# Second block: the S5 mixer ahead of block attention in the side stream, block attention's inputs as plain fp32 products, its gates in a ring slot

## The chip, the cores and the metric

One NeuronCore of a Trainium2 chip runs the whole program. The metric is the device time of one execution in microseconds. The kernel before was timed in three runs.

## The reference, cut to what matters

Two transformer layers (the first block) are followed by one second block; all is fp32, with 256 rows of 1024. The change lies in the second block's mixer:

```python
proj = x @ w_in                               # 1024 -> 1792 RWKV + 1536 MoBA + 512 S5 + 3 x 1024 gates
y_a = rwkv7_mixer(proj[..., :OFF_MOBA], ...)  # a recurrence over 256 positions, 8 heads of 64
y_b = moba_attention(q, k, v)                 # 8 heads; one block of 256, so causal attention with ALiBi
y_c = s5_mixer(proj[..., OFF_SSM:OFF_GATE], ...)   # 32 groups, complex diagonal recurrence, then a GLU
gates = sigmoid(proj[..., OFF_GATE:] + gate_b)     # three gates of 1024 columns
merged = g_rwkv * (y_a @ w_up_rwkv) + g_moba * (y_b @ w_up_moba) + g_ssm * (y_c @ w_up_ssm)
y = merged @ w_out
```

After it come a layer norm, a router and 32 experts.

## The kernel before, in words

For the second block each engine runs three programs woven into one list (`weave`, L149): the RWKV stream, the side stream and a stream of gates ahead. The weaver takes one step (up to a `yield STEP`) of each in turn, in this order; I call that a round and count rounds from the second block's first input product. The list is fixed when the program is built, and every engine works it off strictly in order, so an instruction that waits holds up all behind it. PSUM banks 0 to 3 belong to RWKV, 4 to 6 to the side stream, 7 to the gates.

**Input products.** `proj` is computed in pieces of 256 columns (1 MB of weights). Thirteen are split products, the units (`units_tensor`): ACT writes a rounded copy of the weights (L291), DVE the remainder (L301), and PE multiplies in three passes (L242 to L244). They are the 7 RWKV pieces and the 6 of block attention (queries and keys by columns, values by rows), one a round in rounds 1 to 13. Gates, S5's two input pieces and the products up from a branch are plain fp32 products (`product_cols`, L266).

**Weights.** Every piece is loaded by SP into a ring of `RING` = 4 slots (`WeightRing`). Piece n waits for the use of piece n - 4.

**RWKV.** Its vectors are made beside the units: DVE L1990 to L2013 with exponentials on ACT (L1933, L1937). `b` and `k` (L2005, L2006) wait for a unit whose weights lay in the same memory; `bend` and `kend` (L2012, L2013) follow the last exponential. Then the scan goes over two tiles t of 128 positions: transposes (L2068) in rounds 14 to 17, G with the pair masks (L2074 to L2077, DVE L2232) in 18 to 21, a triangular inverse by products per head (L2045) up to round 33, four steps (L2140 to L2148) in 35 to 38, the chunks (L2159), the output. Tile 1 does the same in rounds 44 to 73. The last product up (RWKV's) and the output product (L736) follow.

**Side stream.** After the units comes block attention in rounds 14 to 27, two groups of four heads: scores (L2379), DVE mask and maximum (L2416, L2423, L2430), exponential on ACT (L887), transposes (L900), the product with the values (L1106). Its product up is in rounds 28 and 29. S5 has its inputs in rounds 30 and 31 and its preparation in 32 to 35: small DVE rows L2640 to L2674 and four transposed pairs (L2524). Eight parts of three rounds each follow, to round 60. For a part, ACT makes an angle (L2575), POOL turns it into the period (L2488, L2490), ACT takes sine and cosine (L2582 to L2587); PE multiplies in (L2510); DVE rotates (call it A, L2688 to L2695), scans (B, L2703) and rotates back (C, L2707 to L2712); PE multiplies out (L2544). The GLU, S5's gates and its product up end the stream in round 67.

**Gates ahead.** After 13 empty steps, block attention's gates run in rounds 14 to 17 and RWKV's in 18, 21, 24 and 27; ACT reads each with a sigmoid (L1801). The result of block attention's stands in `merged`, RWKV's in its own tile.

**POOL** shifts the RWKV inputs (L1627 to L1631) beside the units, then makes distances, pair masks (a memset and 56 selects, L349), `time` and `number`; when block attention is over, it issues S5's loads (L84) and then its part of the angles.

## Time and profile before

| what | us |
|---|---|
| three runs: median (lowest to highest) | 1974.78 (1971.98 to 1976.24) |
| profiled execution, its own time | 1968.7 |
| its span, first to last instruction | 1967.5 |
| busy over the span: PE, DVE, ACT, POOL | 1535.4, 1113.0, 732.7, 147.4 |
| first unit of the second block to first gate | 985 to 1100 |
| block attention and its product up (rounds 14 to 29) | 1099 to about 1220 |
| S5's preparation, parts, then gates and product up | 1241 to 1459 |
| RWKV alone, then the output product and experts | 1462 to the end |

PE is the busiest engine, at a mean granted clock of 0.871. In the timeline each row is a run of like instructions on one engine: its start, its length, line and operation, and in brackets how long the engine had stood idle before it, with the instruction that released it. What ends an idle stretch is read there; busy time alone does not tell it.

### The profile page before, as it was taken

The page shows a single profiled execution, that of the slowest core. Times are in us where ns is not written, and L with a number is a line of the kernel's source. Part 1 is how long each engine was busy: PE and PEld are TensorE (multiplying, and loading weights), DVE is VectorE, ACT ScalarE, POOL GpSimd, SP SyncE. Part 2 cuts the span into 40 slices and gives each one's busy share as a digit, 9 for nine tenths or more (in the row PEclk, how much of TensorE's full clock was granted, in tenths as well). Part 3 has the DMA queues.
Part 4 walks back from the last instruction along what each step waited for, and adds up shares of the span by engine and source line. Part 5 has one row for each costly group of instructions (what it writes and reads, how often), then busy time and mean ns, then how long its engine had stood idle before and what let it go on. Part 6 is the DMA issues. An engine that isn't in the chain of part 4 may idle for free. (4 is left out here: it accounts for less than half of the span.)

```text
span 1967.5 us, 21292 instructions
## 1 busy us (share of the span) xinstructions
PE 1535.4 (78%) x8755; PEld 1276.7 (65%) x8755; DVE 1113.0 (57%) x1457; ACT 732.7 (37%) x926; POOL 147.4 (7%) x226
## 2 busy tenths in 40 slices
PE   2963465999696436899878989787896559999995
PEld 2952455999595335799777878645784446666663
DVE  6756635656675662544456341588124467676675
ACT  2302324444332340554344322332200146666661
POOL 2000001000100000000078000121001000000000
PEclk9975777999797668999989989778987779999997
DMA  8960014878582002555443313100222329999971
GB/s 302 348 241 0 1 44 171 280 250 292 167 285 66 0 0 86 172 173 196 146 121 116 120 65 97 44 1 0 86 86 68 128 86 338 343 344 344 343 296 64
DMA packets 134567, 310.30 MB, mean 158 GB/s; under 512 B 6223, under 2 KB 99750, under 8 KB 114886
## 3 DMA queue, kind: packets, MB, share of 16 engines
q1 hardware_dynamic: 130310, 299.18, 43.3%
q0 software_dynamic: 3584, 8.71, 1.7%
q8 instruction: 69, 1.13, 0.2%
q10 hardware_dynamic: 576, 1.05, 0.2%
q14 instruction: 28, 0.23, 0.0%
HBM read 307.87 MB, written 1.05 MB: 157 GB/s over the span
## 5 line engine op out<-in xcount | busy, mean ns | idle before, releaser
L301 DVE TENSOR_TENSOR mlp_weights_lo<-weights,mlp_weights_hi 128x2048 fp32r<-128x2048 f32 x64 | 146.3, 2291 | 55.9 <-ACT mlp_weights_hi L291 55.9
L242 PE MATMUL bank<-mlp_in_hi,mlp_weights_hi 128*128 128x256 f32 x512 | 147.2, 288 | 14.9 <-DVE mlp_weights_lo L301 14.9
L3177 DVE TENSOR_TENSOR expert_pair_lo<-weights,expert_pair_hi 128x2048 fp32r<-128x2048 f32 x53 | 119.9, 2290 | 64.0 <-ACT expert_pair_hi L3168 64.0
L243 PE MATMUL bank<-mlp_in_lo,mlp_weights_hi 128*128 128x256 f32 x512 | 146.7, 286 | 0.0
L244 PE MATMUL bank<-mlp_in_hi,mlp_weights_lo 128*128 128x256 f32 x512 | 146.6, 286 | 0.0
L291 ACT ACTIVATE mlp_weights_hi<-weights 128x2048 fp32r<-128x2048 f32 x64 | 121.8, 1910 | 49.7 <-issue 44.4
L242 PE MATMUL bank<-expert_pair_hi,x_block_hi 128*128 128x512 f32 x280 | 114.0, 407 | 5.3 <-issue 5.3
L242 PEld LDWEIGHTS bank<-mlp_in_hi,mlp_weights_hi 128*128 128x128 f32 x512 | 100.2, 196 | 16.7 <-DVE mlp_weights_lo L301 15.7
L244 PE MATMUL bank<-expert_pair_hi,x_block_lo 128*128 128x512 f32 x280 | 110.2, 393 | 0.0
L243 PE MATMUL bank<-expert_pair_lo,x_block_hi 128*128 128x512 f32 x280 | 110.0, 393 | 0.0
L266 PE MATMUL bank<-hT,weights 128*128 128x256 f32 x448 | 101.7, 386 | 0.7 <-ACT merged L1801 0.6
L243 PEld LDWEIGHTS bank<-mlp_in_lo,mlp_weights_hi 128*128 128x128 f32 x512 | 100.3, 196 | 1.1
L244 PEld LDWEIGHTS bank<-mlp_in_hi,mlp_weights_lo 128*128 128x128 f32 x512 | 100.0, 195 | 0.0
L242 PE MATMUL bank<-mlp_weights_hi,hidden_hi 128*128 128x512 f32 x256 | 100.0, 391 | 0.0
L243 PE MATMUL bank<-mlp_weights_lo,hidden_hi 128*128 128x512 f32 x256 | 100.0, 390 | 0.0
L244 PE MATMUL bank<-mlp_weights_hi,hidden_lo 128*128 128x512 f32 x256 | 99.6, 389 | 0.0
L538 DVE SCALAR_TENSOR_TENSOR ada<-weights,cond,ada 128x2048 f32<-128x2048 f32 x42 | 98.6, 2347 | 1.4
L3168 ACT ACTIVATE expert_pair_hi<-weights 128x2048 fp32r<-128x2048 f32 x53 | 99.2, 1907 | 0.0
L266 PEld LDWEIGHTS bank<-hT,weights 128*128 128x128 f32 x448 | 85.1, 192 | 14.0 <-issue 2.2
L855 DVE TENSOR_TENSOR hidden_lo<-mlp_raw,hidden_hi 128x512 fp32r<-128x512 f32 x32 | 22.1, 692 | 98.1 <-ACT hidden_hi L831 98.1
L3281 DVE TENSOR_TENSOR y_sorted<-bank,y_sorted 128x512 f32 (+1 forms) x70 | 48.4, 692 | 46.1 <-PE bank L3213 45.7
L825 ACT ACTIVATE mlp_raw<-bank 128x512 f32<-128x512 f32 x32 | 19.1, 598 | 126.3 <-PE bank L244 126.3
(728 smaller groups left out, 3760.9 us busy)
## 6 DMA issues: line engine op xcount, KB each, us to landing
weights<-in_w_ada SPq DMA_DIRECT2D x48, 1024.0 KB, 5.3
weights<-in_w_in SPq DMA_DIRECT2D x45, 1024.0 KB, 5.5
weights<-in_expert_w_gate SPq DMA_DIRECT2D x35, 1024.0 KB, 5.6
weights<-in_w_up SPq DMA_DIRECT2D x32, 1024.0 KB, 5.5
weights<-in_w_down SPq DMA_DIRECT2D x32, 1024.0 KB, 6.0
weights<-in_expert_w_up SPq DMA_DIRECT2D x18, 1024.0 KB, 6.9
weights<-in_expert_w_down SPq DMA_DIRECT2D x18, 1024.0 KB, 7.3
expert_raw<-in_expert_w_up SPq DMA_DIRECT2D x17, 1024.0 KB, 6.6
```

What stands on the lines that cost most here:

```text
L242: pe.e.matmul(out, lhsT[0], rhs[0], start=start, stop=False)
L243: pe.e.matmul(out, lhsT[0], rhs[1], start=False, stop=False)
L244: return pe.e.matmul(out, lhsT[1], rhs[0], start=False, stop=stop)
L266: ins = pe.e.matmul(bank[:, j * SEQ:(j + 1) * SEQ], w[:, k, j * P:(j + 1) * P], xT[:, k, :], start=k == 0, stop=k == tiles - 1)
L291: act.e.activation(self.of(n)[0], ring.view(name), ACT.Copy).then_inc(*act.mark(*self.key, "high", n))
L301: dve.e.tensor_tensor(lo, ring.view(name), hi.bitcast(F32), SUB).then_inc(*dve.mark(*self.key, "low", n))
L538: dve.e.scalar_tensor_tensor(part, ring.view(name), s.cond[:, k:k + 1], part, MULT, ADD).then_inc(*dve.mark(*name))
L825: act.e.activation(s.raw, as_cols(c.up_banks.of("up", l, n)), ACT.Relu).then_inc(*act.mark("read", "up", l, n))
L855: dve.e.tensor_tensor(lo, s.raw, hi.bitcast(F32), SUB).then_inc(*dve.mark("hidden low", l, n))
L3168: act.e.activation(pair[0][:, :, i * D_EXPERT:(i + 1) * D_EXPERT], expert_raw(s, kind, n), ACT.Copy).then_inc(*act.mark("expert", "high", ...
L3177: dve.e.tensor_tensor(pair[1][:, :, part], expert_raw(s, kind, n), pair[0][:, :, part].bitcast(F32), SUB).then_inc(*dve.mark("expert", "lo ...
L3281: dve.e.tensor_tensor(part, c.banks[4 + 2 * (n % 2) + half].unsqueeze(1), part, ADD).then_inc(*dve.mark("expert", "added", n, half))
```

## The change

S5 becomes the first user of the side stream. The units are now 9, the 7 of RWKV and the 2 of S5. S5's preparation takes rounds 10 to 12, its first product in is in 13, and its eight parts end in round 36, beside scan tile 0. GLU and product up are in rounds 37 to 40. The six inputs of block attention are plain fp32 products from the ring, rounds 41 to 46, and block attention runs in rounds 47 to 60 beside scan tile 1, its product up in 61 and 62. From round 63 on RWKV is alone. All twelve gates go ahead in the order S5, RWKV, block attention, one in every second round from 10 to 32. S5's stand in `merged`; block attention's stand in ring slot 3, which the ring gives away at the last unit and goes on with 3 slots. POOL issues S5's loads after the first shift group, makes `time` and `number` before the shifts, the pair masks between its angle parts 0 and 1, the distances after S5. `b` and `k` wait for unit 7 instead of 11. The experts' loads also wait for the last product merged from block attention. In the changed program lines stand lower: L266 becomes L275, L2524 L2552, L2510 L2538, L2544 L2571, L1801 L1820, L2068 L2087, L349 L365, L2488 L2516.

```diff
...
-        self.order.append((name, piece))
+        slot = self.free.pop(0)
+        self.free.append(slot)
+        self.place[name] = slot, len(self.pieces_of[slot]), piece
+        self.pieces_of[slot].append(name)
+        self.order.append(name)
+    def give(self, slot):
+        self.free.remove(slot)
+        return self.pieces_of[slot][-1]
     def view(self, name):
...
-        return self.order[n][1][0](self.slots[n % RING])
+        slot, _, piece = self.place[name]
+        return piece[0](self.slots[slot])
...
-            if n >= RING:
-                yield from sp.wait_ge("used", *self.order[n - RING][0])
-            sp.e.dma_start(view(self.slots[n % RING]), source).then_inc(self.full[n % RING], 16)
-            n += 1
+            name = self.order[done]
+            slot, n, (view, source) = self.place[name]
+            if n:
+                yield from sp.wait_ge("used", *self.pieces_of[slot][n - 1])
+            sp.e.dma_start(view(self.slots[slot]), source).then_inc(self.full[slot], 16)
...
@@ -1586,13 +1602,17 @@
     return pieces
-def second_constants_gpsimd(c, s):
+def distances_gpsimd(c, s):
     pool = c.join.pool
     for t in range(TT):
         pool.e.iota(s.distance[:, t, :], pattern=[[-1, SEQ]], base=t * P, channel_multiplier=1,
                     allow_small_or_imprecise_dtypes=True).then_inc(*pool.mark())
         select(pool, s.distance[:, t, :], ALU.is_ge, 1e34, t * P, [[-1, SEQ]], 1)
...
+def pair_masks_gpsimd(c, s):
+    pool = c.join.pool
     pool.e.memset(s.pair, 1.0).then_inc(*pool.mark())
     for kind, block in ((0, C), (1, C), (2, C), (3, 16), (4, 16)):
...
+    pool.also("pair masks")
...
     pool.e.memset(s.chunk_start.rearrange("p (n c) -> p n c", c=C)[:, :, 0:1], 0.0).then_inc(*pool.mark("chunk starts"))
+    pool.e.iota(s.time, pattern=[[1, SEQ]], base=0, channel_multiplier=0,
+                allow_small_or_imprecise_dtypes=True).then_inc(*pool.mark())
+    pool.e.iota(s.number, pattern=[[0, 1]], base=0, channel_multiplier=1).then_inc(*pool.mark("numbers"))
...
@@ -1629,6 +1650,8 @@
             pool.e.tensor_scalar(s.shift_tmp, s.shift_tmp, s.v["rwkv_mu_2"][:, k:k + 1], None, MULT).then_inc(*pool.mark())
             pool.wait_own()
             pool.e.tensor_tensor(shifted[k], s.shift_tmp, s.z[:, k, 1:SEQ + 1], ADD).then_inc(*pool.mark("rw shifted", k))
+        if n == 0:
+            s5_loads_gpsimd(c, s)
...
-    s.input_weights = Pairs(c, c.join, ("in 2",), s.pieces["rwkv"] + s.pieces["moba"], s.input_pairs)
+    s.input_weights = Pairs(c, c.join, ("in 2",), s.pieces["rwkv"] + s.pieces["ssm"], s.input_pairs)
...
@@ -1706,9 +1729,7 @@
 def input_units(s):
-    return [*((COLS, s.z[:, 2 * n:2 * n + 2, 1:SEQ + 1]) for n in RWKV_ORDER),
-            *((COLS, s.qkT[:, 2 * n:2 * n + 2, :]) for n in range(4)),
-            *((ROWS, s.mb_v[:, :, 256 * n:256 * n + 256]) for n in range(2))]
+    return [*(s.z[:, 2 * n:2 * n + 2, 1:SEQ + 1] for n in RWKV_ORDER), *(s.u[:, 2 * n:2 * n + 2, :] for n in range(2))]
...
 def units_vector(c, s):
+    s.gates_after = c.ring.give(RING - 1)
...
     dve.e.tensor_copy(s.chunk_decay.rearrange("p k n -> p (k n)"), chunks(s.rw_work)[:, :, C - 1]).then_inc(*dve.mark("rw log", "inverse"))
     yield STEP
     yield STEP
-    yield from dve.wait_ge("in 2", "product", 11)
+    yield from dve.wait_ge("in 2", "product", 7)
     yield from dve.wait_ge("rw exp", "inverse")
...
         yield STEP
     dve.wait_own()
-    yield from dve.wait_ge("second constants")
+    yield from dve.wait_ge("pair masks")
...
-    yield from add_branch_vector(c, s, dve, banks, 0, 2, s.rwkv_gates, s.b[:, 0:2, :])
...
+    yield from add_branch_vector(c, s, dve, banks, 0, 1, s.rwkv_gates, s.b[:, 0:2, :])
...
+    s.mb_pT, s.mb_tmp = mem.new("mb_pT", 4, 2, SEQ), mem.new("mb_tmp", 2, SEQ)
+    s.mb_gates = k_tiles(8)(c.ring.slots[RING - 1])
...
+    return [*((COLS, s.qkT[:, 2 * n:2 * n + 2, :]) for n in range(4)), *((ROWS, s.mb_v[:, :, 256 * n:256 * n + 256]) for n in range(2))]
...
+def moba_inputs_tensor(c, s):
+    pe, banks = c.side.pe, c.side_banks
+    for n, (kind, _) in enumerate(moba_inputs(s)):
+        name = "mb in", n
+        c.ring.next(name, s.pieces["moba"][n])
+        yield from c.ring.wait_ge(pe, name)
+        bank = yield from banks.take(pe, *name)
+        product = product_cols if kind == COLS else product_rows
+        product(pe, bank, c.hT, c.ring.view(name), KT).then_inc(*pe.mark(*name))
+        pe.also("used", *name)
+        yield STEP
...
@@ -2455,32 +2502,13 @@
...
 def s5_angles_gpsimd(c, s):
     pool = c.start.pool
     for part in range(8):
+        if part == 1:
+            pair_masks_gpsimd(c, s)
...
-    yield from pe.wait_ge("read", "s5 u", 1)
-    yield STEP
+    yield from pe.wait_ge("read", "in 2", 8)
     yield from s5_in_tensor(s, pe, banks, 0)
...
@@ -2750,62 +2777,59 @@
 def side_branches_tensor(c, s):
     pe, banks = c.side.pe, c.side_banks
     yield from units_tensor(c, s)
+    yield from s5_tensor(c, s)
+    yield from add_branch_tensor(c, s, pe, banks, 2, s.s5_yT)
+    yield from meet(c, "tensor", "s5", "side")
+    yield from moba_inputs_tensor(c, s)
+    for n in range(4):
+        yield from pe.wait_ge("read", "mb in", n)
     for h0 in (0, 4):
         yield from moba_tensor(c, s, h0)
     yield from add_branch_tensor(c, s, pe, banks, 1, s.mb_yT)
-    yield from meet(c, "tensor", "moba", "side")
-    yield from s5_u_tensor(c, s)
-    yield from s5_tensor(c, s)
-    yield from gates_tensor(c, s, pe, banks, 2)
-    yield from add_branch_tensor(c, s, pe, banks, 2, s.s5_yT)
...
-    yield from meet(c, "scalar", "moba", "side")
-    yield from s5_u_scalar(c, s)
-    yield from s5_scalar(c, s)
-    yield from act.wait_ge("branch", 2)
-    yield from gates_scalar(c, s, act, banks, 2, s.s5_gates)
...
 def side_branches_vector(c, s):
     dve, banks = c.side.dve, c.side_banks
     yield from units_vector(c, s)
+    yield from s5_vector(c, s)
+    yield from add_branch_vector(c, s, dve, banks, 2, None, s.merged, None)
+    yield from meet(c, "vector", "s5", "side")
+    for n in range(6):
+        yield STEP
     for h0 in (0, 4):
         yield from moba_vector(c, s, h0)
-    yield from add_branch_vector(c, s, dve, banks, 1, None, s.merged, None)
-    yield from meet(c, "vector", "moba", "side")
-    for n in range(2):
-        yield STEP
-    yield from s5_vector(c, s)
-    for n in range(4):
-        yield STEP
-    yield from add_branch_vector(c, s, dve, banks, 2, 1, s.s5_gates, s.s5_tmp)
...
-AHEAD_STEPS = 13
+    yield from add_branch_vector(c, s, dve, banks, 1, 2, s.mb_gates, s.mb_tmp)
+AHEAD_STEPS, SPACES = 9, 1
...
 def gates_ahead_tensor(c, s):
     for _ in range(AHEAD_STEPS):
         yield STEP
-    for branch, spaces in ((1, 0), (0, 2)):
-        yield from gates_tensor(c, s, c.ahead.pe, c.ahead_banks, branch, spaces)
+    for branch in (2, 0, 1):
+        yield from gates_tensor(c, s, c.ahead.pe, c.ahead_banks, branch, SPACES)
 def gates_ahead_scalar(c, s):
+    act = c.ahead.act
     for _ in range(AHEAD_STEPS):
         yield STEP
-    for branch, gates, spaces in ((1, s.merged, 0), (0, s.rwkv_gates, 2)):
-        yield from gates_scalar(c, s, c.ahead.act, c.ahead_banks, branch, gates, spaces)
+    for branch, gates in ((2, s.merged), (0, s.rwkv_gates), (1, s.mb_gates)):
+        if branch == 1:
+            yield from act.wait_ge("used", *s.gates_after)
+        yield from gates_scalar(c, s, act, c.ahead_banks, branch, gates, SPACES)
...
 def expert_loads_sync(c, s):
     sp, ring = c.start.sp, c.ring
     sources = {kind: c.a[f"expert_w_{kind}_2"].rearrange("a e (p k) n -> (a e) p (k n)", p=P) for kind in KINDS}
-    for name, _ in ring.order[-RING:]:
-        yield from sp.wait_ge("used", *name)
+    for names in ring.pieces_of:
+        yield from sp.wait_ge("used", *names[-1])
+    yield from sp.wait_ge("merged", 1, 6)
...
     yield from shifts_gpsimd(c, s)
-    second_constants_gpsimd(c, s)
-    yield from meet(c, "gpsimd", "moba", "side")
-    s5_loads_gpsimd(c, s)
     yield from s5_angles_gpsimd(c, s)
+    yield from meet(c, "gpsimd", "s5", "side")
+    distances_gpsimd(c, s)
```

Three places show how the lists move. On PE, the rows behind the last unit before (mb_qkT are queries and keys; L2068 is RWKV's first transpose; L266 a gate):

```order
L2068 MATMUL bank0<-identity,rw_AR_324 128x128 [waits rw_scalar,rw_vector,rw_tensor]
L2068 MATMUL bank0<-identity,rw_AR_324 128x128 x3
L2379 MATMUL bank5<-mb_qkT_359 128x128 [waits join_scalar]
L2379 MATMUL bank5<-mb_qkT_359 128x128
L2379 MATMUL bank6<-mb_qkT_359 128x128 [waits join_scalar]
L2379 MATMUL bank6<-mb_qkT_359 128x128
L266 MATMUL bank7<-hT_49,weights1 128x256 [waits weights1_full]
L266 MATMUL bank7<-hT_49,weights1 128x256 x15
L2068 MATMUL bank1<-identity,rw_bend_327 128x128 x4
L266 MATMUL bank7<-hT_49,weights2 128x256 [waits ahead_scalar,weights2_full]
```

And the rows behind the last unit in the changed program (s5_bb and s5_cc are S5's matrices, L2538 its product in):

```order
L275 MATMUL bank7<-hT_49,weights0 128x256 [waits weights0_full]
L275 MATMUL bank7<-hT_49,weights0 128x256 x15
L2552 MATMUL bank4<-identity,s5_bb0_388 128x128 [waits join_scalar,side_vector]
L2552 MATMUL bank4<-identity,s5_bb0_388 128x128 x3
L2552 MATMUL bank5<-identity,s5_bb1_389 128x128 [waits join_scalar]
L2552 MATMUL bank5<-identity,s5_bb1_389 128x128 x3
L2552 MATMUL bank6<-identity,s5_cc0_391 128x128 [waits join_scalar]
L2552 MATMUL bank6<-identity,s5_cc0_391 128x128 x3
L2552 MATMUL bank4<-identity,s5_cc1_392 128x128 [waits side_scalar]
L2552 MATMUL bank4<-identity,s5_cc1_392 128x128 x3
L275 MATMUL bank7<-hT_49,weights1 128x256 [waits ahead_scalar,weights1_full]
L275 MATMUL bank7<-hT_49,weights1 128x256 x15
L2538 MATMUL bank5<-s5_u_367,s5_bT0_380 128x256 [waits side_scalar]
L2538 MATMUL bank6<-s5_u_367,s5_bT1_381 128x256
L2538 MATMUL bank5<-s5_u_367,s5_bT0_380 128x256 [waits side_tensor]
L2538 MATMUL bank6<-s5_u_367,s5_bT1_381 128x256
L2087 MATMUL bank0<-identity,rw_AR_324 128x128 [waits rw_vector,rw_scalar,rw_tensor,side_tensor]
```

Between a gate and RWKV's first transpose there now stand S5's transposes, a second gate and its first products in, each with a wait of its own.

On ACT, the same place in the changed program (L2627 reads S5's transposes, L1956 is RWKV's last exponential, L2602 the angle, L2609 to L2614 sine and cosine):

```order
L2627 ACTIVATE s5_cT1_383<-bank4 128x512 [waits side_tensor]
L1820 ACT_TABLE_LOAD
L1820 ACTIVATE merged_251<-bank7,columns_247 128x256 [waits ahead_tensor]
L1820 ACTIVATE merged_251<-bank7,columns_247 128x256
L1956 ACT_TABLE_LOAD
L1956 ACTIVATE rw_work_355<-rw_work_355 128x1024 [waits rw_vector]
L2602 ACTIVATE distance_241<-time_244,s5_th_370 128x256 [waits side_vector]
L2602 ACTIVATE distance_241<-time_244,s5_th_370 128x256
L2609 ACT_TABLE_LOAD
L2609 ACTIVATE s5_sin0_401<-distance_241 128x512 [waits start_gpsimd]
L2610 ACTIVATE s5_cos0_402<-distance_241 128x512
L2612 ACTIVATE s5_cos0_402<-s5_cos0_402 128x512 [waits side_scalar]
L2614 ACTIVATE s5_cos0_402<-s5_cos0_402,ones 128x512 [waits side_scalar]
L2201 ACTIVATE scan_W_333<-bank0 128x8x64 [waits rw_scalar,rw_tensor,rw_vector]
```

Before, L1937 (now L1956) stood ahead of the first gate's read; now it stands behind the second, and S5's first angle behind it.

On POOL, the rows behind the shifts before:

```order
L1592 IOTA distance_241 128x256
L349 AFFINE_SELECT distance_241<-distance_241 128x256 [waits join_gpsimd]
L1596 MEMSET pair_masks_242 128x640
L349 AFFINE_SELECT pair_masks_242<-pair_masks_242 128x32 [waits join_gpsimd] x24
L349 AFFINE_SELECT pair_masks_242<-pair_masks_242 128x16 [waits join_gpsimd] x32
L1609 IOTA time_244 128x256
L1611 IOTA number_245 128x1
L84 DMA s5_b_re_383<-in_ssm_b_re_2 128x16x16 [waits side_scalar,side_vector,side_tensor]
L84 DMA s5_b_im_384<-in_ssm_b_im_2 128x16x16
...
L2488 TENSOR_SCALAR s5_sin0_400<-distance_241 128x512 [waits side_scalar]
```

and in the changed program:

```order
L2516 TENSOR_SCALAR s5_sin0_401<-distance_241 128x512 [waits side_scalar]
L2518 TENSOR_TENSOR distance_241<-distance_241,s5_sin0_401 128x512 [waits start_gpsimd]
L1616 MEMSET pair_masks_242 128x640
L365 AFFINE_SELECT pair_masks_242<-pair_masks_242 128x32 [waits join_gpsimd] x24
L365 AFFINE_SELECT pair_masks_242<-pair_masks_242 128x16 [waits join_gpsimd] x32
L2516 TENSOR_SCALAR chunk_start_243<-distance_241 128x512 [waits side_scalar]
L2518 TENSOR_TENSOR distance_241<-distance_241,chunk_start_243 128x512 [waits start_gpsimd]
```

The pair masks now stand between the two angle parts instead of ahead of all of S5's work.

## Rows read from the trace of the kernel before

**Rows 1.** Windows: stretch, length, busy us (instructions) PE, PEld, DVE, ACT, POOL, clock, DMA.

```profile
1072.00:1099.00 27.00, 23.80 (x192) 23.19 (x193) 17.21 (x13) 11.29 (x11) 13.77 (x32) 1.00 0.51 157
1099.00:1244.00 145.00, 134.51 (x752) 118.33 (x752) 43.94 (x99) 41.24 (x85) 3.90 (x4) 0.94 0.30 91
1261.00:1386.00 125.00, 100.10 (x600) 66.51 (x600) 100.42 (x163) 37.30 (x65) 26.04 (x16) 0.75 0.00 1
```

**Rows 2.** Timeline of PE: first chunk product of scan tile 1 (start us, us, what).

```profile
1462.18 1.79 PE L2159 MATMUL bank<-scan_state,scan_N 128*128 128x64 f32 x8 [1.49 <-DVE scan_N L2283]
```

**Rows 3.** Timeline of ACT: results of units 8 and 12 read.

```profile
1071.72 0.60 ACT L1765 ACTIVATE mb_qkT<-bank 128x512 f32<-128x512 f32 x1 [1.34 <-PE bank L244]
...
1097.58 0.60 ACT L1765 ACTIVATE mb_v<-bank 128x512 f32<-128x512 f32 x1 [1.04 <-PE bank L244]
```

**Rows 4.** Timeline of PE: two plain products, of block attention's and of RWKV's gates.

```profile
1100.24 8.86 PE L266 MATMUL bank<-hT,weights 128*128 128x256 f32 x32
...
1135.79 7.17 PE L266 MATMUL bank<-hT,weights 128*128 128x256 f32 x32
```

**Rows 5.** Timelines of DVE and PE: first and last row of S5's preparation.

```profile
1240.91 0.17 DVE L2640 TENSOR_TENSOR s_mag<-columns,s_dt 128x16 f32<-128x16 f32 x1
...
1254.18 0.61 DVE L2674 TENSOR_SCALAR s_cc<-s_c_im,group_odd 128x256 f32<-128x256 f32 x2
...
1254.85 1.97 PE L2524 MATMUL bank<-identity,s_bb 128*128 128x128 f32 x8 [7.92 <-DVE s_cc L2674]
```

**Rows 6.** Timeline of ACT: the last exponential, a gate's read, a table load.

```profile
1095.47 1.06 ACT L1937 ACTIVATE rw_work<-rw_work 128x1024 f32<-128x1024 f32 x1 [3.05 <-DVE rw_work L2008]
...
1109.14 0.84 ACT L1801 ACTIVATE merged<-bank,columns 128x256 f32<-128x256 f32 x2 [7.46 <-PE bank L266]
1109.99 1.28 ACT L887 ACT_TABLE_LOAD   x1
1111.29 0.40 ACT L887 ACTIVATE mb_scores<-mb_scores,mb_negmax 128x128 f32<-128x128 f32 x1
```

**Rows 7.** Timelines of ACT and POOL: the first angle, turn and last cosine.

```profile
1260.05 0.90 ACT L2575 ACTIVATE distance<-time,s_th 128x256 f32<-128x256 f32 x2
...
1263.05 1.26 POOL L2490 TENSOR_TENSOR distance<-distance,s_sin 128x512 f32<-128x512 f32 x1
...
1266.19 0.72 ACT L2587 ACTIVATE s_cos<-s_cos,ones 128x512 f32<-128x512 f32 x1
```

**Rows 8.** Timeline of DVE: A's first row, C's first and last row; kend.

```profile
1281.97 0.69 DVE L2688 TENSOR_TENSOR s_br<-bank,chunk_start 128x512 f32<-128x512 f32 x1
...
1289.99 0.68 DVE L2707 TENSOR_TENSOR s_br<-chunk_start,s_gr 128x512 f32<-128x512 f32 x1
...
1292.03 0.69 DVE L2712 TENSOR_TENSOR s_gi<-chunk_start,s_gi 128x512 f32<-128x512 f32 x1
...
1097.71 1.22 DVE L2013 TENSOR_TENSOR rw_kend<-rw_k_in,rw_work 128x1024 f32<-128x1024 f32 x1
```

**Rows 9.** Timeline of PE: a part's products out and in, at either clock.

```profile
1280.43 1.06 PE L2544 MATMUL bank<-s_br,s_cT 128*32 128x256 f32 x2 [3.85 <-DVE s_gi L2712]
...
1353.42 0.62 PE L2544 MATMUL bank<-s_br,s_cT 128*32 128x256 f32 x2
...
1361.71 2.31 PE L2510 MATMUL bank<-s_u,s_bT 32*128 32x256 f32 x8
```

**Rows 10.** Timeline of PE: a scan product per head, at either clock.

```profile
1349.91 3.58 PE L2045 MATMUL bank<-scan_N,scan_PP 128*128 128x128 f32 x16 [6.36 <-DVE scan_N L2247]
...
1356.15 2.05 PE L2045 MATMUL bank<-scan_PP,scan_N 128*128 128x128 f32 x16
```

**Rows 11.** Timeline of PE: transposes of block attention, second group.

```profile
1191.36 1.10 PE L900 MATMUL bank<-identity,mb_scores 128*128 128x128 f32 x8 [3.02 <-DVE mb_scores L2430]
```

**Rows 12.** Instructions of line L349: duration ns min/median/max, first and last start us.

```profile
L349 POOL TENSOR_SCALAR_AFFINE_SELECT pair_masks<-pair_masks x56: 198/212/2532, 1059.3 to 1087.2; 128x16 f32<-128x16 f32 x32, 128x32 f32<-128x32 f32 x24
```

**Rows 13.** Page, DMA issues: KB each, us to landing.

```profile
weights<-in_w_in SPq DMA_DIRECT2D x45, 1024.0 KB, 5.5
```

More of the change, by code:

```diff
@@ L267, in product_cols, with product_rows @@
                               start=k == 0, stop=k == tiles - 1)
+    return ins
+def product_rows(pe, bank, xT, w, tiles, width=256):
+    for t in range(TT):
+        for k in range(tiles):
+            ins = pe.e.matmul(bank[:, t * width:(t + 1) * width], xT[:, k, t * P:(t + 1) * P], w[:, k, :], start=k == 0, stop=k == tiles - 1)
     return ins
@@ L1660, in group_odd_vector @@
     dve = c.side.dve
[L1661 removed]
+    yield from dve.wait_ge("numbers")
     dve.e.tensor_scalar(s.number, s.number, 4, 1, ALU.arith_shift_right, ALU.bitwise_and).then_inc(*dve.mark())
@@ L1758, in units_scalar @@
     act, units = c.join.act, input_units(s)
-    for n, (kind, dst) in enumerate(units):
+    for n, dst in enumerate(units):
         if n + 1 < len(units):
@@ L2228, in scan_vector @@
     dve.wait_own()
-    yield from dve.wait_ge("second constants")
+    yield from dve.wait_ge("pair masks")
     for h in range(HEADS):
@@ L2457, in s5_memory @@
     s.glu = [mem.new(f"s5_glu{n}", 4, SEQ) for n in range(2)]
-    s.s5_gates, s.s5_tmp = mem.new("s5_gates", 8, SEQ), mem.new("s5_tmp", 2, SEQ)
-def s5_u_tensor(c, s):
-    pe, banks = c.side.pe, c.side_banks
-    for n in range(2):
-        name = "s5 u", n
-        c.ring.next(name, s.pieces["ssm"][n])
-        yield from c.ring.wait_ge(pe, name)
-        bank = yield from banks.take(pe, *name)
-        product_cols(pe, bank, c.hT, c.ring.view(name), KT).then_inc(*pe.mark(*name))
-        pe.also("used", *name)
-        yield STEP
-def s5_u_scalar(c, s):
-    act = c.side.act
-    for n in range(2):
-        yield from act.wait_ge("s5 u", n)
-        act.e.activation(s.u[:, 2 * n:2 * n + 2, :], as_cols(c.side_banks.of("s5 u", n)), ACT.Copy).then_inc(*act.mark("read", "s5 u", n))
-        yield STEP
 def s5_angles_gpsimd(c, s):
@@ L2602, in s5_scalar @@
     yield from act.wait_ge("s5 cycles")
-    yield from act.wait_ge("second constants")
+    yield from act.wait_ge("numbers")
     yield from act.wait_ge("rw run")
```

58 lines of the change are left out of this document (28 added, 30 removed).

## The prediction, made before the changed kernel was run

> **What bounds the kernel now.** I read the windows by stage first, then PE's timeline from the first gate to the last chunk, then what ended each wait there. While gates stand beside the scan and block attention, PE is full: 134.5 of 145 us, clock 0.94 [rows 1]. Beside S5's parts it isn't: 100.1 of 125 us, clock 0.75, with DVE as busy as PE. There PE waits for C, DVE's last rows of a part, before it can multiply out (idle 3.85 [rows 9]), and its own rows take longer: a product per head 3.58 us against 2.05 [rows 10]. So the change has a target: some 25 us of holes and as much of low clock beside S5, which gates could fill. The scan's last tile starts its chunks at 1462.2 [rows 2]; what follows stays as it is. I sum from the reading of unit 8, 1071.7 [rows 3], to that first chunk: 390.5 us before. A measurement of this kernel tells a difference of about 0.2%, 4 us.
>
> **Rounds 10 to 13: 44.7 us.** Before, four units took from 1071.7 to 1097.6 and the transposes began at 1099.0. Now: a gate, 7.1 us [rows 4], to 1078.8. S5's preparation waits on DVE for the last unit and takes 13.9 us [rows 5]; DVE also has RWKV's rows there, 8.0 us in 27 when I take four remainders of 2.3 from 17.2 [rows 1], and I lay 3 of them in between. PE's transposes start at 1088.8: 10 us idle. They take 3.3, the next gate ends at 1100.0 (the first after a pause took 8.86). ACT stands before that gate's result, and RWKV's last exponential and S5's first angle stand behind it: read 0.84, table 1.28, exponential 1.06 [rows 6], angle 0.9, POOL's turn 3.4, sines 2.6 [rows 7]: 1110.1. On DVE A(0), 3.8, then bend and kend, 1.2 each [rows 8]: 1116.4. PE has 4 us of S5 in this time and is idle for 12. Round 14 begins 17.4 us later than before. Below, this could be 8 (if the preparation's small rows slip between RWKV's and the exponential isn't late); above, 22.
>
> **Rounds 14 to 36: 187 us.** PE's work: ten gates 71; eight products out of 2.7 and seven in of 2.3 [rows 9], 38; the scan's twelve products per head and eight groups about as long, 20 x 1.95, 39 (one alone 2.05 [rows 10]). That is 148. The holes: out(p) stands on PE behind the RWKV product of its round, and on DVE C(p) stands behind the row that takes this product. So a wait as long as RWKV's row and C, whose four rows take 2.7 [rows 8], comes after that product whether or not a gate ran a round earlier; the trace has one of 3.85 [rows 9]. Further, in(p+1) waits for A(p), A(p) for the sines, the sines on ACT for the gate's read: 0.84 + 1.28 + 2.6 + 3.8 = 8.5 us after a gate's end, against 6 of scan work. Together up to 5.5 a part. The nearest rows, S5's parts now, show 25 idle us for some eight parts, 3.1 each. I take 4, 32 in all, and 7 for rounds 34 to 36, where no gate is left: 39. Ends: 25 and 55.
>
> **Rounds 37 to 46: 89 us.** GLU, product up, six plain inputs: ten plain products, 71, and nine groups of scan, 18. PE is full here. Against split products the six cost PE more (7.1 against 23.8/4 = 5.95 [rows 1, 4]: +7); S5's two are cheaper by 2. DVE loses four remainders of 2.3 and ACT four copies, but neither bounds.
>
> **Rounds 47 to 60: 62 us.** Block attention and scan tile 1 are now without gates. PE has some 36 us of work, 2.6 a round. Before, a round here took 6.9 (145 us for 21), 4.1 of it plain products (twelve of 7.1). Even so PE waited 3.02 for DVE's masked scores [rows 11]. With nothing to fill, each round lasts as long as its chain: product, DVE, ACT, back. I take 4.4, between 2.6 (36 us) and 6.9 (97), nearer to 3.0 plus a wait in every second round.
>
> **Rounds 61 to the chunk: 32 us.** Two halves up, 14.2, with scan rows 3.7; then G's last products and steps, 13.9, RWKV alone.
>
> Sum 44.7 + 187 + 89 + 62 + 32 = 414.7, against 390.5: +24. The clock: PE now rests in rounds 47 to 60 as it rested beside S5. If a third of 36 us of work runs at 3.58 for 2.05, that is 9 more; the first holes give 2. RWKV rows on DVE that POOL's selects held up before give 3 back. **+32 us.** Against the profiled execution, 1968.7, it is 2001; the median of the runs shown is 6 above it, so I say 2006.
>
> **What costs nothing.** S5's four loads on POOL delay its shifts by 4 us, or up to 9 if each waits its turn; the shifts are followed by 28 us of masks now [rows 12], which move away. Three slots instead of four: a load lands 5.5 us after issue [rows 13] and has at least one product of 7.1 for cover; without it, 5.5 at most twice. SP's experts wait for the last merge of block attention, about 14 us before the chunk.
>
> **A page's rule.** A table load took 1.28 us, and the next activation began 0.02 after its end [rows 6]. The Trainium skill, "ScalarE: Activation LUTs", section "What ACT_TABLE_LOAD costs", adds a drain of about 1.38 us to every switch of set. The program gains ten loads; by the page ten drains, an estimate of 14 us, would come on top; by the row none does, so I leave it out.
>
> **Rivals.** (B) **Faster, 0.22.** Gates and S5 fit: DVE is through C before PE asks, since a gate of 7.1 us lies in between. For it: 93% busy in 1099 to 1244 with gates, and S5's rows are shorter at full clock. Against: C behind RWKV's row of the same round. It decides when the idle per part falls under 1 us and block attention's round under 3.6: rounds 14 to 36 then take 160, rounds 47 to 60 50, rounds 10 to 13 35: 49 us less than my sum, 1957. With no hole at all the work is 22 + 148 + 89 + 36 + 32 = 327, and the time 1911. (C) **About the same, 0.06**: half of the holes I laid fill, 1975. (D) **POOL's masks stand in the way, 0.17.** They start behind turn 0, at about 1107.5, and take 12 (56 at the median 0.212) to 28 us (as before, beside DVE, the longest 2.5 each) [rows 12]. Angle 1's turn stands behind them: to 1139 at worst, while A(1) is wanted near 1130; PE then loses up to 11: 2017. The Trainium skill, "GPSIMD Engine Reference", section "Key points", has GpSimd share its SBUF interfaces with VectorE and contend with two-input instructions; the longest select is twelve times the median, which agrees. (E) **A ring of three makes pieces late, 0.05**: some 5 us for several pieces, 2015 to 2025. The forecast itself has 0.5.
>
> **Chances.** Faster by over 0.2%: B, 0.22 and a share of C. Same: 0.06. Slower: the forecast, D, E. The range reaches up to D with the holes' upper end, 2034, and down into B, to 1945, which leaves out its best cases.
>
> **What would show it.** Right: PE idle about 10 us before S5's transposes and 12 before the first RWKV transpose; idle of 3 to 5 us before products out, released by C; rounds 47 to 60 around 60 us at a low clock; first chunk of tile 1 near 1071.7 + 423. Wrong: this stretch at or below 390; S5's parts over 90% busy on PE; the masks' end as what releases PE; a wait for weights in the chain.

## The result and the profile after

The changed kernel takes 2017.84 us (median of four, 2014.21 to 2024.99); the kernel before 1975.51 in the same comparison. The ratio is 1.0216, interval 1.0178 to 1.0255: slower, by 42 us. The forecast was 2006, slower, range 1945 to 2034.

The profiled execution took 2014.21 us, its span 2012.6 against 1967.5. What answers to the sum of the prediction, by its own stages, are the windows of the changed kernel (stretch, length, busy us and instructions of PE, PEld, DVE, ACT, POOL, clock, DMA); the last row runs from the first unit to the first chunk of scan tile 1:

```profile
1068.90:1113.40 44.50, 20.21 (x88) 16.86 (x88) 22.79 (x61) 19.35 (x28) 10.90 (x25) 0.74 0.15 48
1113.40:1325.30 211.90, 173.51 (x914) 130.15 (x914) 96.23 (x154) 60.68 (x96) 31.44 (x49) 0.83 0.16 50
1325.30:1413.60 88.30, 83.81 (x530) 73.27 (x529) 10.45 (x18) 12.04 (x21) 1.45 (x4) 0.96 0.34 108
1413.60:1479.70 66.10, 43.74 (x321) 40.08 (x321) 36.65 (x78) 18.07 (x50) 0.00 (x0) 0.79 0.05 17
1479.70:1506.60 26.90, 26.12 (x338) 23.97 (x336) 12.84 (x23) 2.34 (x5) 0.00 (x0) 1.00 0.23 79
993.00:1506.60 513.60, 412.82 (x2649) 343.95 (x2649) 225.46 (x368) 142.31 (x234) 98.07 (x130) 0.86 0.22 70
```

The same stretch of the kernel before:

```profile
996.50:1462.20 465.70, 404.50 (x2714) 338.75 (x2714) 232.82 (x372) 137.61 (x230) 104.87 (x130) 0.90 0.24 76
```

It is 47.9 us longer. PE is busy 8.3 us more and idle 39.6 us more (100.8 against 61.2). Of the idle time 21.9 us more lie ahead of RWKV's first transpose (34.8 against 12.8) and 17.7 behind it. If each busy moment is weighted with the clock granted in it, PE's work is 367.5 us against 365.8, an estimate from the two traces: most of the 8.3 is a lower clock, hardly any of it more work. The rest of the program is as before: 506.0 us from the chunk to the end of the span, 505.3 before. PE's timeline in the changed kernel, in order: S5's first transposes, RWKV's first transpose, the gate behind it, products out of parts 0, 1, 2 (the row of 1174.42 stands between, a product in) and 7, transposes of block attention, first chunk:

```profile
1085.64 1.97 PE L2552 MATMUL bank<-identity,s_bb 128*128 128x128 f32 x8 [9.85 <-DVE s_cc L2701]
...
1113.40 1.09 PE L2087 MATMUL bank<-identity,rw_AR 128*128 128x128 f32 x4 [14.38 <-DVE rw_kend L2032]
...
1118.67 10.01 PE L275 MATMUL bank<-hT,weights 128*128 128x256 f32 x32
...
1132.56 1.06 PE L2571 MATMUL bank<-s_br,s_cT 128*32 128x256 f32 x2 [3.44 <-DVE s_gi L2739]
...
1155.72 1.06 PE L2571 MATMUL bank<-s_br,s_cT 128*32 128x256 f32 x2 [5.58 <-DVE s_gi L2739]
...
1174.42 4.17 PE L2538 MATMUL bank<-s_u,s_bT 32*128 32x256 f32 x8 [3.43 <-DVE s_gr L2719]
...
1193.18 1.06 PE L2571 MATMUL bank<-s_br,s_cT 128*32 128x256 f32 x2 [3.67 <-DVE s_gi L2739]
...
1319.98 1.06 PE L2571 MATMUL bank<-s_br,s_cT 128*32 128x256 f32 x2 [10.50 <-DVE s_gi L2739]
...
1441.26 1.97 PE L916 MATMUL bank<-identity,mb_scores 128*128 128x128 f32 x8 [11.49 <-DVE mb_scores L2477]
...
1506.62 1.87 PE L2178 MATMUL bank<-scan_state,scan_N 128*128 128x64 f32 x8
```

Every wait shown is for a row of DVE. What DVE waited for in rounds 10 to 13 stands in its own timeline (before these two rows it made b and k and the input of RWKV's last exponential, up to 1089.2) and in ACT's:

```profile
1107.03 0.69 DVE L2715 TENSOR_TENSOR s_br<-bank,s_cos 128x512 f32<-128x512 f32 x1 [17.83 <-ACT s_cos L2614]
...
1111.92 1.23 DVE L2032 TENSOR_TENSOR rw_kend<-rw_k_in,rw_work 128x1024 f32<-128x1024 f32 x1
```

```profile
1096.82 0.84 ACT L1820 ACTIVATE merged<-bank,columns 128x256 f32<-128x256 f32 x2 [5.57 <-PE bank L275]
1097.68 1.28 ACT L1956 ACT_TABLE_LOAD   x1
1098.97 1.06 ACT L1956 ACTIVATE rw_work<-rw_work 128x1024 f32<-128x1024 f32 x1
1099.93 0.89 ACT L2602 ACTIVATE distance<-time,s_th 128x256 f32<-128x256 f32 x2
```

DVE stands still for 17.8 us before A(0), with bend and kend behind it. ACT is held up by the gate's read to 1097.7, and behind that come exponential, angle, turn and sines, 9.4 us. The table load at 1097.68 is followed by its activation 0.01 us after its end, as in [rows 6].

### The profile page after: what moved, and what is told of

Same layout as the page of the kernel before. It is cut to its first block, busy times and chain, and to the rows that moved or that the text cites. A ratio compares the mean times of both kernels' runs of the same rounds, so it can differ in the third digit from the quotient of the medians.

```text
span 2012.6 us, 21151 instructions
## 1 busy us (share of the span) xinstructions
PE 1542.5 (77%) x8691; PEld 1280.2 (64%) x8691; DVE 1105.3 (55%) x1453; ACT 738.8 (37%) x932; POOL 140.5 (7%) x226
## 4 chain that ended last, share of the span: by engine, by line
PE 70%; DVE 21%; ACT 6%; issue 2%; DMA 0%; POOL 0%; DVEq 0%; ACTq 0%
PE bank L251 12%; PE bank L252 12%; PE bank L253 12%; PE bank L275 8%; PE bank L3238 6%; PE bank L752 4%; PE bank L2064 2%; PE bank L2571 2%; DVE ada L554 2%; PE bank L499 1%; PE bank L2538 1%; PE bank L608 1%; DVE conv L1332 1%; PE bank L916 1%; ACT diff_scores L903 1%
## 5 line engine op out<-in xcount | busy, mean ns | idle before, releaser
L275 PE MATMUL bank<-hT,weights 128*128 128x256 f32 x512 | 124.4, 405 | 0.2
L275 PEld LDWEIGHTS bank<-hT,weights 128*128 128x128 f32 x512 | 103.4, 205 | 20.4 <-PE bank L2538 3.1
L251 PEld LDWEIGHTS bank<-mlp_in_hi,mlp_weights_hi 128*128 128x128 f32 x512 | 100.2, 196 | 16.7 <-DVE mlp_weights_lo L317 15.7
L3306 DVE TENSOR_TENSOR y_sorted<-bank,y_sorted 128x512 f32 (+1 forms) x70 | 48.4, 692 | 46.2 <-PE bank L3238 44.5
```

The lines of the kernel that those rows point to most:

```text
L251: pe.e.matmul(out, lhsT[0], rhs[0], start=start, stop=False)
L275: ins = pe.e.matmul(bank[:, j * SEQ:(j + 1) * SEQ], w[:, k, j * P:(j + 1) * P], xT[:, k, :], start=k == 0, stop=k == tiles - 1)
L3306: dve.e.tensor_tensor(part, c.banks[4 + 2 * (n % 2) + half].unsqueeze(1), part, ADD).then_inc(*dve.mark("expert", "added", n, half))
```

## The experiments

The start of the second block drifts: its first unit began between 993 and 1012 us, whatever the kernel. The stretch from it to tile 1's first chunk does not; in the two kernels that differ only in POOL's masks it is 513.6 both times. So I read the experiments by that stretch, from one profile each, cut at RWKV's first transpose, and give the ratio beside it. The part up to the transpose agrees within 0.3 us in the six kernels that leave PE, ACT and DVE there as in the changed one (120.3 to 120.6), and in the four with plain inputs in the old order it is 100.1 to 100.2. Behind the chunk it takes 504.1 to 509.0 us to the end of the span, so a gain of a few us in the stretch need not be one of the program. None of the ratios of the seven kernels built on the changed one but that of gates_spread has an interval apart from the changed kernel's; for all others what the edit is worth rests on the stretch alone.

| kernel | to transpose | to chunk | sum | ratio to before (interval) |
|---|---|---|---|---|
| before | 102.6 | 363.2 | 465.7 | 1 |
| changed | 120.4 | 393.2 | 513.6 | 1.0216 (1.0178 to 1.0255) |
| masks_early | 120.3 | 393.3 | 513.6 | 1.0246 (1.0221 to 1.0272) |
| gates_from_14 | 111.4 | 399.2 | 510.6 | 1.0230 (1.0205 to 1.0255) |
| s5_one_round_later | 100.9 | 410.9 | 511.9 | 1.0228 (1.0195 to 1.0260) |
| side_first_dve | 120.6 | 391.0 | 511.6 | 1.0257 (1.0235 to 1.0279) |
| filled_waits | 120.3 | 396.7 | 517.0 | 1.0265 (1.0243 to 1.0287) |
| filled_where_idle | 120.4 | 386.4 | 506.8 | 1.0193 (1.0156 to 1.0231) |
| gates_spread | 120.5 | 403.9 | 524.4 | 1.0304 (1.0272 to 1.0336) |
| plain_inputs_only | 100.1 | 358.8 | 458.9 | 0.9988 (0.9964 to 1.0012) |
| s5_gates_beside_s5 | 102.6 | 359.3 | 461.9 | 0.9992 (0.9973 to 1.0012) |
| plain_and_s5_gates | 100.2 | 357.9 | 458.1 | 0.9971 (0.9944 to 0.9998) |
| both_and_filled | 100.2 | 360.6 | 460.8 | 0.9984 (0.9963 to 1.0005) |
| side_first_s5_only | 100.1 | 364.4 | 464.5 | 0.9997 (0.9980 to 1.0014) |

**masks_early**: on the changed kernel.

```diff
-        if part == 1:
-            pair_masks_gpsimd(c, s)
...
     yield from shifts_gpsimd(c, s)
+    pair_masks_gpsimd(c, s)
     yield from s5_angles_gpsimd(c, s)
```

> The changed kernel with the pair masks made on POOL right after the shifts, ahead of S5's first angle. In the changed kernel's trace they take 19.2 us between turn 0 and turn 1, and turn 1 ends at 1127.3. Chain theory: they are mostly hidden, since sine 1 stands on ACT behind a gate's read anyway; 0 to 3 us faster than the changed kernel, ratio 1.020 to 1.0216. Rival (the masks hold up turn 1 and with it the whole chain of parts): 8 to 11 us faster, 1.016 to 1.0175.

The stretch is the same to 0.1 us, and so are the waits before the products out (3.43, 5.58, 3.66, 3.43, 10.49). Rival D falls: the masks are hidden. In the changed kernel POOL has

```profile
1104.85 19.24 POOL L365 TENSOR_SCALAR_AFFINE_SELECT pair_masks<-pair_masks 128x32 f32<-128x32 f32 x56
```

against some 28 us [rows 12].

**gates_from_14**: the gates four rounds later.

```diff
-AHEAD_STEPS, SPACES = 9, 1
+AHEAD_STEPS, SPACES = 13, 1
```

> The changed kernel with all twelve gates four rounds later (rounds 14, 16 ... 36 instead of 10 ... 32). Chain theory (what costs time are waits between engines, not PE's work): ACT no longer stands before a gate's result while RWKV's last exponential and S5's first angle wait behind it, so the first RWKV transpose comes 10 to 14 us earlier after the last unit (31 to 34 us behind it instead of 44.5); the two gates that move to rounds 34 and 36 cost 14 us of work there and fill 7 to 10 us of the idle 10.5 before the last product out. Sum: 7 to 10 us faster than the changed kernel, ratio to the kernel before about 1.017. Rival (PE's work is the bound, the order of gates does not matter): no change, 1.0216.

The start gains 9.0 us and the later rounds lose 6.0: 3 us in all, not 7 to 10. What left the start is PE's work (busy 74.9 instead of 85.6 us); its idle time there did not fall, 36.5 for 34.8. Right in direction; two gates in rounds 34 and 36 fill less than I gave them (the last wait is 6.0 instead of 10.5).

**s5_one_round_later**: the same idea driven further; the new step stands in S5's program on PE, ACT and DVE alike, ahead of part 0.

```diff
-AHEAD_STEPS, SPACES = 9, 1
+AHEAD_STEPS, SPACES = 14, 1
...
     for n in range(4):
         yield from dve.wait_ge("read", "s5 T", n)
+    yield STEP
     for part in range(8):
```

> The changed kernel with S5's parts one round later and the gates from round 15 on, so that on ACT no gate's result stands before RWKV's last exponential, and on DVE bend and kend stand ahead of A(0). Chain theory: the first RWKV transpose comes 18 us earlier (first unit to transpose 102 instead of 120.4: only S5's preparation, 14 us of small DVE rows, then b, k, bend, kend and one exponential are left); from there to tile 1's first chunk it takes 400 to 404 instead of 393.2 (two gates more, most of rounds 34 to 37 filled). First unit to chunk 502 to 506 against 513.6. Rival (what the start gains comes back as waits between the parts, as with the gates four rounds later): 510 or more.

The start comes out as said, 100.9: kend comes 19.5 us earlier when ACT's queue and A(0) are not ahead of it. But 17.7 of them come back, 1.7 are left. The rival holds. Why, PE's timeline and window behind the last unit show:

```profile
1096.48 1.97 PE L2552 MATMUL bank<-identity,s_bb 128*128 128x128 f32 x8 [16.75 <-DVE s_cc L2703]
...
1104.92 0.87 PE L2087 MATMUL bank<-identity,rw_AR 128*128 128x128 f32 x3 [4.76 <-DVE rw_kend L2032]
```

```profile
1079.70:1104.90 25.20, 3.70 (x17) 3.28 (x17) 19.48 (x55) 9.94 (x16) 2.27 (x1) 0.59 0.00 0
```

Of these 25.2 us PE is idle for 21.5; in the changed kernel it was 24.3 of 44.5. So the edit moved two gates and the first product in out of this stage, to where they had to be done later, and hardly touched the holes: kend's wait is 4.8 instead of 14.4, but s_cc's is 16.8 instead of 9.9. It shows what sets the length of the stage. It does not show that the stage's holes are harmless, and no run here took them away.

**side_first_dve**: DVE's streams swapped after 14 rounds.

```diff
-    yield from weave(rwkv_branch_vector(c, s), side_branches_vector(c, s))
+    yield from weave_then_swap(14, rwkv_branch_vector(c, s), side_branches_vector(c, s))
```

> The changed kernel with the two streams on DVE in the other order from round 14 on: in each round S5's (or block attention's) rows stand ahead of RWKV's. Chain theory: C(p) no longer stands behind the row that takes RWKV's product of the same round, so the idle time of PE before a product out falls from 3.4 to 5.6 us to 0 to 2; RWKV's rows come 2.7 to 3.9 us later and take some of it back. 5 to 12 us faster than the changed kernel, ratio 1.0155 to 1.019. Rival (C follows the scans B closely and its own length is what PE waits for): idle before products out unchanged, no change or slower by up to 10.

Two waits before products out are left (1.86, 5.42), and from the first transpose to the last product out it takes 199.9 instead of 211.9 us. So C's place behind RWKV's row is what PE waits for. But beside block attention the same swap costs 8.3 us (101.3 for 93.0): RWKV's product then waits for its operand. 2 us are left of 5 to 12.

**filled_waits** and **filled_where_idle**: extra products ahead of the wait. They add work whose result is overwritten by the product out.

```diff
-        yield from pe.wait_ge("s5 h", part)
         bank = yield from banks.take(pe, "s5 out", part)
+        for _ in range(FILL[part]):
+            pe.e.matmul(bank[:, 0:SEQ], c.identity, c.hT[:, 0, :], start=True, stop=True)
+        yield from pe.wait_ge("s5 h", part)
```

`FILL` is 8 everywhere in the first, (7, 7, 7, 7, 0, 0, 0, 7) in the second.

> The changed kernel with eight extra plain 256-column products (identity times hT, into the bank that the part's product out then overwrites) ahead of each wait for C, 64 in all; 0.22 us each at full clock, 1.8 us a part. Clock theory: rounds 14 to 36 cost 25 us more than their work at full clock, because PE rests before each product out and is granted 1.2 GHz behind it; with the rests filled the clock stays up and the rows behind them shorten by 8 to 20 us; the extra products lie in time that was idle. 8 to 18 us faster than the changed kernel, ratio 1.0125 to 1.0175. Rival (the low clock follows from something else, or the extra products push C's successors back): no change, or up to 14 us slower (64 x 0.22).

> The changed kernel with seven extra plain products (3.2 us at full clock) only before the products out of parts 0 to 3 and 7, where PE stood idle for 3.4 to 10.5 us; the run with extra products in all eight parts had them at 3.7 us each, products out at 2.7 instead of 4.1 to 4.9 behind them, and lost 11 us in parts 4 to 6 that had no idle time. Clock theory: rounds 14 to 36 take 212 - 7 = 205 us (5 times 2 less, some of the waits a little over-filled), stretch 431 to 434. Rival (the clock does not matter at these places): 438 and no change.

In all parts: 3.4 us more, since three parts had no wait and paid 3.7 each. Where PE did wait: 6.8 us less, and 205.1 us from transpose to last product out, as expected. The timeline of filled_where_idle at part 0 shows it: the wait of 3.44 is 0.41 after the extra products, and a pair of products out takes 0.62 instead of 1.06.

```profile
1130.57 3.19 PE L2568 MATMUL bank<-hT,identity 128*128 128x256 f32 x14
...
1134.16 0.62 PE L2573 MATMUL bank<-s_br,s_cT 128*32 128x256 f32 x2 [0.41 <-DVE s_gi L2741]
```

The low clock is thus a cost of its own beside the waits, and 6.8 us of it were got back at five places. How much of the whole loss it is, these runs don't show.

**gates_spread**: fewer gates beside S5, some beside block attention.

```diff
-AHEAD_STEPS, SPACES = 9, 1
+AHEAD_STEPS, SPACES = 9, {2: 1, 0: 5, 1: 3}
...
-        yield from gates_tensor(c, s, c.ahead.pe, c.ahead_banks, branch, SPACES)
+        yield from gates_tensor(c, s, c.ahead.pe, c.ahead_banks, branch, SPACES[branch])
```

> The changed kernel with S5's gates in rounds 10 to 16 as there, RWKV's in 18, 24, 30, 36 and block attention's in 42, 46, 50, 54. Chain theory: the waits before S5's products out and before block attention's transposes are set by DVE and ACT, not by PE's work. Four gates fewer beside S5 shorten rounds 14 to 36 by some 20 us (28 of work, less what they had filled, and the clock is lower); gates in rounds 42 and 46 cost 7 each in full, those in 50 and 54 cost 7 together, since 22 us of idle lie there. Stretch from the last unit to the first chunk of tile 1 about 438 - 20 + 21 = 439 at worst and 430 at best (438 in the changed kernel); ratio 1.018 to 1.022. Rival (the gates fill S5's holes well where they are): 445 or more.

10.8 us worse: the theory missed here. From the first transpose to the last product out it got 22.3 us shorter for five gates fewer, 4.5 each. The full rounds behind got 19.3 longer for three, 6.4 each. And the stretch from the scores to the chunk got 13.7 longer for two gates, 6.9 each, although 22 us of idle lay there; its waits stayed:

```profile
1432.79 7.17 PE L275 MATMUL bank<-hT,weights 128*128 128x256 f32 x32
...
1452.02 1.97 PE L916 MATMUL bank<-identity,mb_scores 128*128 128x128 f32 x8 [10.24 <-DVE mb_scores L2477]
...
1462.94 7.17 PE L275 MATMUL bank<-hT,weights 128*128 128x256 f32 x32
```

The wait of 11.49 is 10.24 with a gate in the round. So here a gate does not go into the wait. DVE's timeline says why:

```profile
1441.06 0.69 DVE L2251 TENSOR_TENSOR scan_G<-bank,pair_masks 128x512 f32<-128x512 f32 x1 [6.28 <-PE bank L2094]
...
1442.66 1.21 DVE L895 TENSOR_REDUCE mb_negmax<-mb_scores 128x4 f32<-128x1024 f32 x1
```

Block attention's scores were multiplied ahead of the gate. But their maximum (L895) stands on DVE behind RWKV's row for G, and G's product stands on PE behind the gate, so DVE waits 6.28 us. From the maximum to the transposes it takes 9.4 us in both kernels (in the changed one from 1431.89). The gate thus delays the start of the chain that ends the wait, through the other stream's row. This is read from the traces, not tried by itself. Measured is the price: beside S5 a gate costs 4.5 of its 7.1 us, beside block attention 6.9. S5 is the better place for them, as the change has it.

**plain_inputs_only** and **s5_gates_beside_s5**: on the kernel before, in its order. In the first the units are RWKV's seven, and block attention's six inputs follow as in the changed kernel; in the second S5's gates run in the ahead stream eight rounds after RWKV's, with five empty rounds between, into the given-away slot.

```diff
-    s.input_weights = Pairs(c, c.join, ("in 2",), s.pieces["rwkv"] + s.pieces["moba"], s.input_pairs)
+    s.input_weights = Pairs(c, c.join, ("in 2",), s.pieces["rwkv"], s.input_pairs)
...
     yield from units_tensor(c, s)
+    yield from moba_inputs_tensor(c, s)
```

```diff
-    yield from gates_tensor(c, s, pe, banks, 2)
     yield from add_branch_tensor(c, s, pe, banks, 2, s.s5_yT)
...
+    for _ in range(LATER):
+        yield STEP
+    s.gates_after = c.ring.give(RING - 1)
+    yield from gates_tensor(c, s, c.ahead.pe, c.ahead_banks, 2, 5)
```

> The kernel before with the other part alone: block attention's six inputs as plain fp32 products from the ring, in the same rounds, units only for RWKV. From its rows: six split units go at 6.5 us each, six plain products at 7.1 to 7.4, so 4 to 5 us slower; DVE loses 14 us and ACT 11 us of work there, which may bring RWKV's vectors forward and give 0 to 4 back. Ratio 1.000 to 1.0025. Rival (the split's remainders on DVE are what delays RWKV's chain at this place): up to 6 us faster.

> The kernel before with one part of the idea: order and units stay, but S5's four gates stand beside S5's parts (rounds 38, 44, 50, 56, kept in the ring's last slot) instead of alone behind the GLU. Chain theory: 28 us of full-clock work goes away in rounds 62 to 65, where RWKV's four steps then wait for DVE (some 8 us of idle); beside S5 each gate costs 7 less 2 to 3 of idle filled and brings some clock back (rows there at 1.2 GHz are some 20 us too long in all). 5 to 15 us faster than the kernel before, ratio 0.992 to 0.9975. Rival 1 (gates never fill S5's waits): 1.004. Rival 2 (all waits fill): 0.987.

Plain inputs were to cost 4 to 5 us; they save 6.8 in the stretch, 2.5 ahead of the first transpose and 4.4 behind it. The rival with DVE's remainders fits: ahead of the transpose PE waited 5.2 us for them in five waits, now 1.8 in one. But with six units fewer b and k also wait for unit 5 instead of 11, and b starts at 1080.05 instead of 1091.82, so the remainders are not the only thing that moved; and the 4.4 us behind the transpose are not explained. The windows up to the transposes (plain inputs, then before) show PE busier and idle 5.3 us instead of 12.8, and DVE relieved of 12.6:

```profile
998.90:1099.00 100.10, 94.83 (x562) 84.36 (x563) 48.89 (x44) 31.43 (x40) 64.64 (x110) 0.96 0.42 129
```

```profile
996.50:1099.00 102.50, 89.67 (x657) 83.02 (x658) 61.47 (x47) 43.19 (x47) 74.93 (x110) 0.94 0.44 137
```

S5's gates beside S5 save 3.8 us of the stretch, below the 5 to 15 expected. Neither ratio can be told from 1.

**plain_and_s5_gates, both_and_filled, side_first_s5_only**: both edits together; then with `FILL` 5 in every part; or with the DVE swap from round 36 to 61 alone (`SWAPS = 35, 61`, the streams reversed after each).

> The kernel before with both parts that were tried alone on it: block attention's inputs plain (first unit to chunk 458.9 against 465.7) and S5's gates beside S5's parts (461.9). If their gains lie in different stretches they add: 455, ratio about 0.995; if both only lift the same low clock, 459 and 0.9985.

> The same with five extra plain products (identity times hT, 2.3 us at full clock) ahead of each wait for C in S5's parts. In the kernel before, PE stands idle there for 0.2 to 3.9 us in six of eight parts, and the clock over S5's parts is 0.75. Clock theory: the extra products keep 2.4 GHz, products out go from 5.0 to 2.7 and in from 4.2 to 2.3, scan rows likewise; they cost up to 1 us a part beyond the idle time. 5 to 15 us less than without them. Rival (in this order DVE is the bound of these parts, 100 of 125 us busy): 0, or up to 10 more.

> The kernel before with plain inputs and S5's gates beside S5 (458.1 us from the first unit to tile 1's first chunk), and on DVE the side stream ahead of RWKV from round 36 to 61, only beside S5's parts. In the changed kernel the same swap took 12.0 us out of the stretch with S5's parts and gave 8.3 back beside block attention. Theory (PE's wait for C is C's place behind RWKV's row): the idle times of 0.9 to 4.3 before products out fall under 1.5, 4 to 10 us less, 448 to 454, ratio 0.992 to 0.995. Rival (beside S5 in this order RWKV's own chunks wait for DVE, and with DVE busy 100 of 125 us one of the two must wait): no change or up to 8 more.

The two edits hardly add: 458.1 against 458.9. It is the only kernel here whose ratio is clear of 1 on the fast side (0.9971, interval to 0.9998), and only just; as one of five such ratios it can be chance. Filling costs 2.7 us although it cut PE's idle time in the stretch from 54.4 to 41.0: this order has waits of 0.9 to 4.3 in six parts. The swap leaves one wait of 0.33 before the products out, and the stretch is 6.4 longer. So in this order the wait before a product out is not what bounds; when it goes, RWKV's rows wait instead.

## Why the prediction was right

The direction held, and so did most of the mechanism: the holes at the start, C and A as what PE waits for, block attention's rounds without filler. One term, the clock beside S5, was far too small; the time came out in the range because it was wide and other terms erred the other way. By its own terms:

| stage | forecast | measured |
|---|---|---|
| rounds 10 to 13 | 44.7 | 44.5 |
| rounds 14 to 36 | 187, 39 of it idle | 211.9, 38.4 idle |
| rounds 37 to 46 | 89 | 88.3 |
| rounds 47 to 60 | 62 | 66.1 |
| rounds 61 to the chunk | 32 | 26.9 |
| clock and masks | +8 | in the rows above |
| sum | 422.7 | 437.7 |

- **Rounds 10 to 13.** Idle 9.85 for s_cc and 14.38 for kend, against 10 and 12. The steps were those named: preparation, gate's read, exponential, angle, turn, sines, A(0), bend, kend. s5_one_round_later shows that those from the gate's read on set when kend comes. The prediction did not ask what a cure would give; moving the gates away gave 1.7 us and left the holes.
- **Rounds 14 to 36.** The idle time was right in sum: waits before the first four products out of 3.4 to 5.6, released by C, and 10.5 at the last; before three products in 3.4 to 3.9, released by A. side_first_dve confirms C's place. But the forecast had a wait before every product out, "whether or not a gate ran a round earlier", and parts 4 to 6 had none; that 39 met 38.4 is in part luck (the last wait was 10.5 and not 7). **The term that was mis-sized is the clock**: "the first holes give 2". PE was busy 173.5 us, clock 0.83; weighted with the clock granted in it that is 145.6 us of work at full speed, an estimate from the trace, so the 148 were counted well and the low clock cost 28. Ten gates took 81.1 instead of 71, the first of them 10.0. The forecast had read the same loss in the kernel before (clock 0.75 beside S5, [rows 1]) and took it to go away with the gates. A hole of 3 to 5 us costs its length and then slow rows behind it. filled_where_idle got back 6.8 us net at five such places. This stage came out 23 us above the forecast with its 2 for the clock; the last two stages came out 10 below theirs (with the 9), and the 3 from the masks are not seen. That makes the 15 us that the sum was short: against the kernel before the forecast said +32 for this sum, and +47 was measured. The whole program moved by 42 and was thus nearer to the forecast than its sum was. In the two profiled executions the second block's first unit began 3.4 us earlier in the changed kernel, which is drift.
- **Rounds 37 to 46**, full of plain products, needed only counting.
- **Rounds 47 to 60.** 66.1 measured is the 62 and half the 9 for clock; 22.4 us idle. In the kernel before, the windows from the first transpose to the product up (1099 to 1206) hold eight gates of 7.1 and 50 us beyond them; now it is 66 us without gates. PE was idle for 8.8 us there and is for 22.4 now; the window before:

```profile
1099.00:1206.00 107.00, 98.20 (x550) 85.70 (x551) 36.10 (x78) 33.48 (x71) 0.00 (x0) 0.92 0.22 70
```

So eight gates seem to have filled some 16 us of this chain (the scan's rows beside it are not quite the same ones), but two, put back by gates_spread, filled almost nothing (6.9 us for each). The forecast did not consider what the gate itself delays; whether the place of the gate makes the difference was not tried.
- **What costs nothing**: the masks (masks_early), three slots (no product of the stretch waits for weights) held, and so did S5's loads: on POOL they take 3.9 us, and the units up to the reading of unit 8 take 75.9 us instead of 75.2. The plain inputs I priced at +7 on PE; alone they save 6.8. Their price in the new order was not tried.
- **The rivals.** B failed where it was to be decided: the idle per part was 4.8, not under 1, and block attention's round took 4.7, not under 3.6. (Its 1957 carries the +8 for clock and masks along, its 1911 does not; without them its sum of 366 gives 1949.) D failed by masks_early, E by the missing waits for weights.

What remains of the cause: with plain inputs and S5's gates moved in the old order the stretch is 458.1, with them in the new order 513.6. The 55 us between belong to the order of the side stream with what hangs on it (S5's units, the rounds of all gates, three slots). They show as 46 us more of idle time on PE and 9 more of busy time. Seven edits of the changed kernel gave back 0 to 7 us or cost 3 and 11. None of them removed the 24 us of holes in rounds 10 to 13, so what these cost stays open. Which pairing of scan tile and mixer costs how much was not separated further.

## What to carry to other kernels

Work of another stream fills a wait only if nothing that ends the wait depends on a product queued behind that work, neither the row itself nor one that stands ahead of it on its engine, as RWKV's row for G did here; before moving filler, follow the wait back to its last product on the same engine. When an edit shortens a stage, look whether its idle time fell or only work left it. A removed wait often comes back in the other stream when both share in-order queues, so price a cure by the whole stretch and not by the wait that it removes. On PE, price a hole of a few microseconds as the hole plus the slower rows behind it.

## What was not expected

- Seven useless products ahead of a wait made the stretch shorter, 506.8 for 513.6 us: the product out began about when it did before and ran at 0.62 us a pair instead of 1.06.
- Block attention's inputs by one-pass plain products beat the three-pass split ones on the whole, though PE's share of each is longer (7.1 against 5.95): 458.9 against 465.7 us. The medians of the whole can't tell it (0.9988, interval 0.9964 to 1.0012).
- A stretch of some 500 us repeated to 0.1 us in the one pair of kernels that could show it, while its start drifted by up to 19; with the parts that agree elsewhere this suggests that one profile of such a stretch can show what medians of the whole can't. The same kernel was not profiled twice.
